# Two mixer layers and an attention stage: values of both mixers computed token-major, gates joined to them

## The reference, cut to what matters

```
h = rmsnorm(x, g)                         # per token: x * g / rms(x)
proj = h @ w_in                           # mqk 1024, mv 1024, mo 1024, mi 4, mf 4,
                                          # aq 1024, ak 256, av 256, ga 1024, gb 1024
mq, mk = silu(causal_conv(mqk));  mv -> 4 heads x 256
ig = mi + b_igate;  logf = log_sigmoid(mf + b_fgate)        # 4 heads each
hm = mlstm_chunkwise(mq, mk, mv, ig, logf)                  # gated linear attention
hm = groupnorm(hm) * sigmoid(mo)
ha = sliding_window_attention(aq, ak, av, sinks, rel_bias)  # 16 query, 4 key/value heads
y  = sigmoid(ga) * (hm @ w_branch_m) + sigmoid(gb) * (ha @ w_branch_a)
return y @ w_out
```

## Time and profile before

| | |
|---|---|
| runs | 2221.68 us median, 2221.55 to 2221.81 (3 runs) |
| profiled execution | span 2219.4 us; its own device time is not listed |
| PE busy | 2177.2 us, 98% |
| DVE, ACT, POOL busy | 1046.4, 1086.0, 973.8 us |
| mean granted clock of PE | 0.995 of full |
| DMA | 198.70 MB, mean 90 GB/s |
| PRE of layer 0 | from the start to 52 us; that of layer 1 from 872 to 908 us |

### The profile page before, as it was taken

How to read it: one execution, slowest core, us unless ns; L and a number is a source line. 1 busy time by engine, 2 the same in 40 slices (tenths; PEclk the granted TensorE clock), 3 DMA queues, 4 the chain that set the end, 5 groups by cost and what they waited for, 6 DMA issues and landing times.

```text
span 2219.4 us, 31509 instructions
## 1 busy us (share of the span) xinstructions
PE 2177.2 (98%) x10287; PEld 1795.8 (81%) x10287; DVE 1046.4 (47%) x2195; ACT 1086.0 (49%) x2273; POOL 973.8 (44%) x757
## 2 busy tenths in 40 slices
PE   7999999999999999999999999999999999999988
PEld 6888888888888888888888788888888787777766
DVE  7365355523132234563563723321324726777773
ACT  6456466434232234464564624322324427787783
POOL 3333333444444544434333444544444424555544
PEclk9999999999999999999999999999999999999999
DMA  4222222223322222222222233223222431221203
GB/s 141 76 86 74 88 86 67 85 95 104 102 97 95 95 95 95 86 76 77 95 72 81 70 101 104 95 95 105 95 95 95 155 124 58 68 68 56 76 30 124
DMA packets 60287, 198.70 MB, mean 90 GB/s; under 512 B 6814, under 2 KB 13519, under 8 KB 59536
## 3 DMA queue, kind: packets, MB, share of 16 engines
q1 hardware_dynamic: 54128, 184.43, 24.9%
q10 hardware_dynamic: 6048, 12.84, 1.6%
HBM read 192.99 MB, written 4.26 MB: 89 GB/s over the span
## 4 chain that ended last, share of the span: by engine, by line
issue 57%; POOL 26%; PE 10%; DVE 4%; ACT 1%; POOLq 1%; DMA 0%; DVEq 0%; SPq 0%; ACTq 0%
POOL w_lo L545 26%; PE ps L643 2%; PE ps L645 2%; PE ps L644 2%; DVE Pn L2220 1%; PE ps L980 1%; PE ps L971 1%; DVE PTn L2236 1%; PE ps L993 1%; POOLq L541 1%; POOLq L543 1%; PE ps L994 1%; DVE y L2207 0%; DVE ocur L2249 0%; PE ps L939 0%
## 5 line engine op out<-in xcount | busy, mean ns | idle before, releaser
L545 POOL TENSOR_TENSOR w_lo<-w_raw,w_hi 128x512 fp32r<-128x512 f32 x592 | 780.0, 1324 | 1054.8 <-ACT w_hi L1060 1052.6
L643 PE MATMUL ps<-hT_hi,w_hi 128*128 128x512 f32 x1600 | 644.8, 403 | 1.7 <-DVE hT_lo L1753 1.2
L645 PE MATMUL ps<-hT_hi,w_lo 128*128 128x512 f32 x1600 | 627.3, 392 | 0.0
L644 PE MATMUL ps<-hT_lo,w_hi 128*128 128x512 f32 x1600 | 626.1, 391 | 0.0
L1060 ACT ACTIVATE w_hi<-w_raw 128x512 fp32r<-128x512 f32 x664 | 411.2, 626 | 411.7 <-PE ps L645 384.2
L645 PEld LDWEIGHTS ps<-hT_hi,w_lo 128*128 128x128 f32 x1600 | 301.6, 189 | 65.6
L643 PEld LDWEIGHTS ps<-hT_hi,w_hi 128*128 128x128 f32 x1600 | 302.2, 189 | 62.1 <-issue 2.4
L644 PEld LDWEIGHTS ps<-hT_lo,w_hi 128*128 128x128 f32 x1600 | 302.8, 189 | 58.0 <-issue 0.5
L643 PE MATMUL ps<-u_hi,w_hi 128*128 128x512 f32 x512 | 199.2, 389 | 0.0
L644 PE MATMUL ps<-u_lo,w_hi 128*128 128x512 f32 x512 | 199.2, 389 | 0.0
L645 PE MATMUL ps<-u_hi,w_lo 128*128 128x512 f32 x512 | 199.2, 389 | 0.0
(11 more groups left out here) (330 smaller groups left out, 3444.6 us busy)
## 6 DMA issues: line engine op xcount, KB each, us to landing
w_raw<-w_all SPq DMA_DIRECT2D x332, 512.0 KB, 3.2
bias<-scr_w ACTq DMA_DIRECT2D x8, 512.0 KB, 3.6
biasn<-scr_n SPq DMA_DIRECT2D x4, 1024.0 KB, 5.4
w1k<-w_in ACTq DMA_DIRECT2D x2, 1024.0 KB, 7.3
w1v<-w_in ACTq DMA_DIRECT2D x1, 2048.0 KB, 12.7
scr_x<-x ACTq DMA_DIRECT2D x1, 2048.0 KB, 7.5
x<-scr_x SPq DMA_DIRECT2D x1, 2048.0 KB, 9.2
out<-x SPq DMA_DIRECT2D x16, 128.0 KB, 1.8
```

The source lines that it names most:

```text
L545: nc.gpsimd.tensor_tensor(w_lo[:, h, :], raw[:, h // 2, (h % 2) * HALF:(h % 2 + 1) * HALF], w_hi[:, h, :].bitcast(F32), ALU.subtract).then ...
L643: nc.tensor.matmul(ps[:, p, :], wh, hi[:, kk, :], start=(kk == 0), stop=False)
L644: nc.tensor.matmul(ps[:, p, :], wh, lo[:, kk, :], start=False, stop=False)
L645: last = nc.tensor.matmul(ps[:, p, :], wl, hi[:, kk, :], start=False, stop=(kk == KT - 1))
```

## The change

Unit counts stay at 140 per layer. Per layer:

- **vg** in place of the v units and of the gates' product: the 256 columns of av and the 8 gate columns form 264 columns (`VW`), packed as two units of four k tiles, 528 columns per half, in a DRAM input of their own (`value_weights` on SP). Now hx is the operand that is loaded and the weights move: 4 token tiles x 8 k x 3 matmuls of 264 columns into banks 2 to 5 (`group_values`). ACT reads the banks out with a per-token factor `rs_tok` (`group_out`) into `vtok` and `gtok`. No transposes.
- **norm0** in place of norm_: it also makes the sum of squares token-major, with four one-column fp32 products into bank 6.
- **GT**: eight transposes turn the gate columns in `gtok` to rows. gate_rows_in, gate_rows and gate_rows_max stand behind all eight tiles on DVE.
- **mx**: the values of heads 0 and 1 (512 columns) from hx, in PRE ahead of conv, four units of 24 matmuls of 512 columns into banks 0 to 3 (`head_values`), read out by ACT into `vbuf[0]` and `vbuf[1]` (`first_pair_out`). The k tiles go in the order 2..7, 0, 1, since `vbuf[1]` lies over the last tiles of hx_lo.
- **mv**: heads 2 and 3 from h, four units in the third turn, into banks 2 to 5 (`second_pair_out`). The other turns have none, and TV is gone.
- The bias tables' small products become a step of their own behind mx 1 in layer 0. hi_parts are called at other steps. The NSA gate weights are 48 columns wide, not padded to 128.

```
+VALUES = unit("vg", 0) + unit("vg", 1)
+PRE_FIRST = (unit("k", 0) + unit("k", 1)[:3] + [("norm0",)] + unit("k", 1)[3:] + VALUES + unit("mx", 0) + [("GT",)] + unit("mx", 1)
+             + [("tables",)] + unit("mx", 2) + [("gatesT",)] + unit("mx", 3) + CONV[0:3])
+PRE_LATER = (unit("k", 0)[:3] + [("norm0",)] + unit("k", 0)[3:] + unit("k", 1) + VALUES + unit("mx", 0) + [("GT",)] + unit("mx", 1)
+             + unit("mx", 2) + [("gatesT",)] + unit("mx", 3) + CONV[0:3])
...
+    return ([("begin",)] + CONV[done:] + unit("conv", 1) + list(values) + unit("q", 0) + [("bc",)] + unit("q", 1)
...
+            def token_products(out, h, k, t, wh, wl, first, final):
+                toks = slice(t * P, (t + 1) * P)
+                nc.tensor.matmul(out, h[0][:, k, toks], wh, start=first, stop=False)
+                nc.tensor.matmul(out, h[1][:, k, toks], wh, start=False, stop=False)
+                return nc.tensor.matmul(out, h[0][:, k, toks], wl, start=False, stop=final)
+            def group_values(s, u, sv, tv):
...
+                for t in range(TT):
+                    last = token_products(ps[:, 2 + t, 0:VW], hx, k, t, wh, wl, k == 0, k == KT - 1)
...
+            def head_values(s, u, h, order, banks, ready):
...
+                for t in (2 * (q % 2), 2 * (q % 2) + 1):
+                    last = token_products(ps[:, banks[t], :], h, order[j], t, wh, wl, j == 0, j == KT - 1)
...
     PE, first mx unit:
+                            cur["mx", "S"] = us[1:3]
+                            for b_ in range(2):
+                                pe.wait_ge(g_free[b_], us[0].m + 1)
+                                pe.wait_ge(s_free[b_], us[1 + b_].m + 1)
...
     ACT:
+            def group_out(u, sv, tv):
+                for t, (ready, free, use) in enumerate(...):
+                    if t == TT - 1:
+                        product(u)
+                        act.sem_inc(ready, 1)
+                    act.wait_ge(ready, use.m + 1)
+                    nc.scalar.activation(vtok[:, :, t, :], ps[:, 2 + t, 0:NG * DH]..., ACT.Copy, scale=rs_tok[:, t:t + 1])
+                    nc.scalar.activation(gtok[:, t, :], ps[:, 2 + t, NG * DH:VW], ACT.Copy, scale=rs_tok[:, t:t + 1]).then_inc(free, 1)
...
+                        if s == ("u1", "vg", 1):
+                            group_out(cur["u"], cur["vg", "S"], cur["vg", "T"])
...
                         gemm_step(s, cur["u"])
...
+                            hi_parts(l, (0, 1) if l == 0 else (2,))
+                        elif s == ("h0", "vg", 0):
+                            hi_parts(l, (2, 3) if l == 0 else (3, 4))
+                        elif s == ("u1", "vg", 0):
+                            hi_parts(l, (4, 5) if l == 0 else (5, 6))
+                        elif s == ("h0", "vg", 1):
+                            hi_parts(l, (6, 7) if l == 0 else (7,))
...
     DVE, behind rs and the stores of k:
+                for k in range(3, KT):
+                    tile(l, k, rs[:, :])
+                    tile_lo(l, k - 1)
+                tile_lo(l, KT - 1)
+                gate_rows_in(pre["GT",])
                 gate_rows()
...
+                gate_rows_max()
```

More of the change, by code:

```diff
@@ L56 @@
 WROW = W0 + 2 * P
+VW = 2 * P + 2 * MH
+VHALF = 2 * VW
+GW = 3 * 16
+RAW_ORDER = tuple((k + 2) % KT for k in range(KT))
 def unit(kind, n):
@@ L507, in _ @@
             first = UNITS - KT - NG * 8 + 2
-            with sp.Fori(0, first // 2 - 1) as i:
+            value_weights(0)
+            with sp.Fori(0, LAYER_UNITS // 2 - 1) as i:
                 for p in range(2):
-                    weights(p, i * 2 + p + 2)
+                    weights(p, i * 2 + p + 4)
+            value_weights(1)
+            with sp.Fori(0, (first - LAYER_UNITS - 4) // 2) as i:
+                for p in range(2):
+                    weights(p, i * 2 + p + LAYER_UNITS + 4)
             sp.wait_ge(hid_done, 1)
@@ L537, in _, with split_pairs @@
         def _(pool):
-            def split_pairs(count, before):
+            def split_pairs(count, before, cols=HALF):
                 with pool.Fori(0, count) as i:
@@ L699, in _ @@
                                 waits=waits and (lambda k: (waits[0], waits[1] + k + 1)))
-                        if l == 0 and s == ("u1", "v", 0):
+                    elif s[0] == "tables":
+                        tables(us)
+                    elif s[0] == "GT":
+                        if l == 0:
                             pe.wait_ge(cst_in, 16 * 5)
[L702 to L709, removed]
+                        for b_ in range(2):
+                            pe.wait_ge(s_free[b_], cur["vg", "S"][b_].m + 2)
+                            pe.wait_ge(t_free[b_], cur["vg", "T"][b_].m + 2)
+                        for n, t_ in enumerate(us):
+                            pe.wait_ge(t_free[t_.b], t_.m + 1)
+                            for t in range(TT):
+                                last = nc.tensor.transpose(ps[0:MH, 4 + t_.b, t * P:(t + 1) * P], gtok[:, t, n * MH:(n + 1) * MH], ident[:, :])
+                            last.then_inc(t_ready[t_.b], 1)
                     elif s[0] == "gatesT":
@@ new lines, in pair_out, with first_pair_out @@
+            def pair_out(t, bank, scale=1.0):
+                nc.scalar.activation(vbuf[0][:, t, 0:MDV], ps[:, bank, 0:MDV], ACT.Copy, scale=scale)
+                return nc.scalar.activation(vbuf[1][:, t, 0:MDV], ps[:, bank, MDV:2 * MDV], ACT.Copy, scale=scale)
+            def first_pair_out(u, sv):
+                for t in range(2):
+                    act.wait_ge(pair_ready, 2 * cur["l"] + t + 1)
+                    act.wait_ge(g_free[t], cur["mx", 2 + t].m + 1)
+                    pair_out(t, t, rs_tok[:, t:t + 1]).then_inc(g_free[t], 1)
+                act.wait_ge(s_ready[0], sv[0].m + 1)
+                pair_out(2, 2, rs_tok[:, 2:3]).then_inc(s_free[0], 1)
+                product(u)
+                act.sem_inc(s_ready[1], 1)
+                pair_out(3, 3, rs_tok[:, 3:4]).then_inc(s_free[1], 1)
@@ new lines, in second_pair_out @@
+            def second_pair_out(u, sv, tv):
+                for t, (ready, free, use) in enumerate(((s_ready[0], s_free[0], sv[0]), (s_ready[1], s_free[1], sv[1]),
+                                                        (t_ready[0], t_free[0], tv[0]), (t_ready[1], t_free[1], tv[1]))):
+                    if t == TT - 1:
+                        product(u)
+                        act.sem_inc(ready, 1)
+                    act.wait_ge(ready, use.m + 1)
+                    pair_out(t, 2 + t).then_inc(free, 1)
@@ L1288, in _ @@
                 act.wait_ge(k_copied, 4 * (l + 1))
+                for b_ in range(2):
+                    act.wait_ge(s_free[b_], cur["vg", "S"][b_].m + 2)
+                    act.wait_ge(t_free[b_], cur["vg", "T"][b_].m + 2)
                 act.wait_ge(h_ready, (l + 1) * KT)
@@ L1635, in store @@
                     last.then_inc(g_free[u.b], 1)
-                elif kind == "v" and cur["layer"]:
-                    product(u)
-                    V.tensor_tensor(vtmp[:, n, :], g, rs[:, :], ALU.mult).then_inc(g_free[u.b], 1)
                 elif kind == "k":
```

382 lines of the change are left out of this document (195 added, 187 removed).

## The result

The changed kernel took **2235.7 us** (median of 4 runs, 2232.3 to 2237.5), the kernel before 2221.6 beside it: ratio 1.0071, 95% interval [1.0059, 1.0083]. It is 0.7% slower, 23 us above the forecast and outside its range. The profiled execution has a span of 2235.6 us (2219.4 before).

A forecast was written before the change was run, and what follows sets the result against it. PE's instruction stream was taken as the bound. 2219.4 us less 14.4 (PE work) and 1.3 (waits), plus 4.1 and 0.9 (stalls) and 1.6 (low clock), gave 2210.3; with 2.3 around the span 2212.6 us, range 2206 to 2218.

The forecast's parts named there:

- the mx and mv units: Value matmuls on PE: same 24 matmuls of 512 columns each as the old mv units, so 0 change.
- the edits that cost nothing: Later gate_rows, bank read-outs, loop turns without mv, smaller gate weights, 3% larger value-weight DMAs: claimed to add no time.
- vg: Added PE work per layer: 96 matmuls of 264 columns at 0.123 us, in all 11.8 us.
- R3: Rival: PE's weight load can't be hidden in vg, 0.19 us per matmul; 2225.5 us, 2228.7 with more clock dips; chance 0.05.
- norm0's small products: Added PE work per layer: four one-column products as eight fp32 passes of 0.117 us, 0.95 us.
- GT: Added PE work per layer: eight transposes onto four partitions, taken as two groups of four, 0.9 us.
- The wait ahead of the first mx unit: Layer 0: PE waits for banks that ACT frees only behind hi_parts and group_out; 4.1 us, bounds 2.5 and 6.5.
- R1: Rival: no stall to speak of, ACT and DVE keep pace in layer 0; 2206.9 us, chance 0.15.
- The slow matmuls behind it: Layer 0, after the wait ahead of mx: PE restarts at the low clock, adding 1.6 us.
- R2: Rival: low clock spreads to GT, norm0 or vg, and POOL lengthens the tile chain by 2 us; 2217.8 us, chance 0.15.
- The forecast's reading of PE's waits: Kernel before: 9.1 us before the first weights, and in both mixer layers only 1.2 us for a tile of h and crumbs.
- R4: Rival: loop turns lose their cushion, turns 1, 2 and 4 of each layer pay 1 us or more; 2218.6 us, chance 0.10.

The follow-up runs named there:

- a_haalign: The changed kernel with weight halves 2304 bytes apart and ha_hi, ha_lo and the last part's tensors 128 bytes higher; 2211.0 us, 0.9958 of the kernel before.
- b_shift64: The kernel before with w_hi and w_lo 64 bytes higher and everything behind them 256 bytes higher; 2260.3 us, ratio 1.0183.
- b_all128: The kernel before with every SBUF tensor, weights and moving operands alike, 128 bytes higher; 2219.6 us, ratio 1.0003.
- c_early: a_haalign with ACT's bank releases earlier and hT copies later ahead of the first mx unit, and one PE wait later; 2202.5 us, 0.9925 of the kernel before.

## Why the prediction was wrong

**The step that failed** is one that the forecast didn't write down as a step. Its sum starts from 2219.4 and moves only by the terms of the changed code, so it puts all the unchanged matmuls at no change, without a reason. It took 0.227 us per matmul of 512 columns from the kernel before, put the mx and mv units at "0", and listed among the edits that cost nothing the larger value weights ("DMAs are 3% larger"), but not what they do to `w_hi` and `w_lo`. Both have other strides in the diff, and every unit of the kernel goes through them. What stood in its place: 3.4 ns on each of some 7600 matmuls, 26 us in the trace. The changed kernel with only the strides put right ran at 2212.8, 23 us less. That this is the forecast's 2212.6 so nearly is in part luck: the kernel before stood 2.3 us lower that time, and the ha tiles still cost some 2 us. By the ratios the change gained 0.26% there and 0.42% with the ha tiles moved too (a_haalign), forecast 0.41%.

**What was right**, by its steps:
- vg: 25.27 to 36.82 are 95 spacings of 0.1216 us, 11.7 us for the 96 (forecast 0.123, 11.8). R3, PE's load as the bound, didn't come. The Trainium skill, "TensorE: Matmul & The Clock Gate", section Back-to-back issue gap, calls its N/2.4 + 2.5 ns an isolated gap; the forecast's estimate from it, 112 ns, is 10 below the 121.6 of this stream, and the measurement decides.
- norm0's small products 0.81 (0.95), GT 0.79 (0.9).
- The wait ahead of the first mx unit 4.14 (4.1), by the mechanism given: ACT's copy of hT tile 7 ended at 39.94 (39.5), group_out behind it. So R1, no stall, didn't come. Timeline of ACT in the changed kernel:

```profile
39.34 0.60 ACT L1274 ACTIVATE hT_hi<-ps 128x512 fp32r<-128x512 f32 x1 [1.08 <-DVE ps L1875]
39.83 0.47 ACT L1284 ACTIVATE vtok<-ps,st 128x256 f32<-128x256 f32 x1
```

- The slow matmuls behind it: from 41.23 to GT at 48.40 are 7.17 us for 24 matmuls, 1.7 over 24 x 0.227 (1.6; the forecast's own rows give 3.75 - 2.05 = 1.7). In layer 1 the wait was 0.6 (0.9). R2, a clock that falls at GT, norm0 or vg too, didn't come: from norm0 to the loop turns the granted clock of the changed kernel was low only behind the 4.1 us wait in layer 0 and behind the gate columns of both layers.
- The forecast's reading of PE's waits passed over the two for Pw in the loop turns, 2.1 us, longer than the 1.2 it named; they stayed, so the sum didn't suffer.
- The loop turns: from the first mqk transpose to the first ha matmul layer 0 fell from 319.75 to 305.54 us (a_haalign, starts in the trace), 14.2 less; two mv units (10.9) and six groups of transposes (2.8) fewer are 13.7. R4 didn't come.
- Both layers together, norm0 to the first u matmul and first hx to the first u: a_haalign's trace is 4.8 and 6.2 us shorter than that of before. The forecast's terms give 2.8 and 6.3, so layer 0 gained 2 us more than said; there a slow stretch after the gate columns that the forecast let stay was missing in a_haalign. The measured ratio, 0.9958 [0.9942, 0.9975], agrees with the 0.41% of the forecast.

**What I had named as signs of being wrong** (spacing of vg, waits in the turns, the size of one wait) watched only the changed code. All of them stayed silent while the kernel came out 1% above the forecast. None looked at the spacing of the unchanged majority, where 1 ns is worth 7.6 us.

What isn't known: why a distance of 64, 128 or 192 bytes costs, why 192 costs 2.2 ns in one stretch and 6.7 in another, and why a transient follows each change of distance. No run shows a mechanism.

## What to carry to other kernels

In a kernel of fp32r matmuls like these, when a diff changes the shape or place of a buffer that the main loop reads, write down the byte address of each operand before and after, though no instruction changes; keep each weight slice and the operand that moves past it at the same address modulo 256, and pad the stride when a slice grows. Compare the spacing of unchanged instructions between two traces before explaining anything else: a PE that is 100% busy at full clock was 3% slower in b_shift64 (233.3 against 226.7 ns). And price a stall by who stands behind whom in an engine's program: moving two copies and the release of a bank in ACT's order, and one wait in PE's, gave 8.5 us, as much as the whole change with its layout put right (8.7).

## What the runs showed of the hardware that I had not expected

- The spacing of back-to-back fp32r matmuls of 512 columns depends on the distance in bytes between weights and moving operand in SBUF, modulo 256: in the MLP 226.7 ns at 0, 233.3 at 64, 232.4 at 128, 228.9 at 192. At 0 the absolute address doesn't count (b_all128). At 128 and 192 it isn't constant within a run: from 412 to 533 us it was 233.3 in both.
- The drop to the low clock after short work isn't the same from run to run. In layer 1 of the kernel before the granted clock was 0.50 from 909 to 911 us, behind the 16 gate matmuls; in b_all128, where only addresses differ, it was 1.00 there (0.23 us from start to start). Behind the same 16 tiny gate matmuls of layer 1 it came in a_haalign and stayed away in c_early (timelines of PE, in that order):

```profile
909.39 1.94 PE L799 MATMUL ps<-ident,grow 4*128 4x4 f32 x16
911.27 0.50 PE L675 MATMUL ps<-w_hi,hx_hi 128*128 128x512 f32 x1
...
912.65 0.63 PE L677 MATMUL ps<-w_lo,hx_hi 128*128 128x512 f32 x1
913.08 0.63 PE L675 MATMUL ps<-w_hi,hx_hi 128*128 128x512 f32 x1
```

```profile
901.40 1.94 PE L801 MATMUL ps<-ident,grow 4*128 4x4 f32 x16
903.27 0.50 PE L675 MATMUL ps<-w_hi,hx_hi 128*128 128x512 f32 x1
...
904.53 0.39 PE L677 MATMUL ps<-w_lo,hx_hi 128*128 128x512 f32 x1
904.76 0.39 PE L675 MATMUL ps<-w_hi,hx_hi 128*128 128x512 f32 x1
```

  The spacing is 0.43 us in the one and 0.23 in the other, the 1.2 and the 2.4 GHz level, 1.6 us over the 24 matmuls behind the gate columns. A single profile can differ from another by a few of these, so layer times are trusted here to 2 us only, and comparisons of whole kernels rest on the medians.
- GT's eight transposes cost no clock in c_early: the matmuls behind 41.82 follow at 0.23 us. The Trainium skill, "TensorE: Matmul & The Clock Gate", section Part 4: PE-mode transpose, says that transposes don't count as PE work for the clock in the same way; with one microsecond of them between long products the trace shows no drop.
